# Two attention heads issued alternately on the two halves of TensorE, and their softmax made two heads ahead

## The reference, cut to what matters

```python
def hybrid_mixer(h, w_in, sink, conv_w, g_attn, g_conv, w_out, cos, sin):
    proj = h @ w_in                                   # 1024 -> 512 q, 128 k, 128 v, 3 x 512 gates
    q, k, v, gate_b, gate_c, u = jnp.split(proj, SPLITS, axis=-1)
    q = partial_rope(q.reshape(b, s, 8, 64), cos, sin)
    k = partial_rope(k.reshape(b, s, 2, 64), cos, sin)
    y_attn = windowed_gqa_with_sink(q, k, v, sink)    # 8 heads of 64, 2 key heads, window 128
    y_conv = gate_b * centred_short_conv(gate_c * u, conv_w)
    y = jnp.concatenate([rmsnorm(y_attn, g_attn), rmsnorm(y_conv, g_conv)], axis=-1)
    return y @ w_out
```

## Time and profile before the change

| what | value |
|---|---|
| median of three runs | 1908.02 us |
| the profiled execution's own time | 1910.71 us |
| its span (first to last instruction) | 1909.0 us |
| TensorE busy over the span | 1840.7 us, 96% |
| VectorE busy | 854.2 us, 45% |
| ScalarE busy | 686.5 us, 36% |
| mean granted TensorE clock | 0.993 |
| first mixer of layer 0, first scores to the sums of squares | 41.45 to 101.06 us |
| first mixer of layer 1, the same | 618.08 to 677.67 us |
| experts of layer 0 and 1, DMA share in their middle | 1.01, at 427 GB/s |

### The profile page before, as it was taken

How to read it: one execution, slowest core, us unless ns; L and a number is a source line. 1 busy time by engine, 2 the same in 40 slices (tenths; PEclk the granted TensorE clock), 3 DMA queues, 4 the chain that set the end, 5 groups by cost and what they waited for, 6 DMA issues and landing times.

```text
span 1909.0 us, 28641 instructions
## 1 busy us (share of the span) xinstructions
PE 1840.7 (96%) x11394; PEld 1248.8 (65%) x11394; DVE 854.2 (45%) x1921; ACT 686.5 (36%) x1319; POOL 277.1 (15%) x249
## 2 busy tenths in 40 slices
PE   8999999999999999999999999999899999999998
PEld 8874444444447874444434436888899978888997
DVE  5863121211215862112211114566785655668755
ACT  5632111111114541111111113557674544576654
POOL 1500000000000500000000003972000057800000
PEclk9999999999999999999999999999999999999999
DMA  8569999999996469999999996452534845433353
GB/s 298 219 263 415 418 428 426 428 428 428 428 424 231 183 280 412 421 427 428 428 428 428 428 427 230 144 207 89 174 97 151 282 169 177 174 132 109 120 169 134
DMA packets 121432, 557.61 MB, mean 292 GB/s; under 512 B 5008, under 2 KB 49584, under 8 KB 96240
## 3 DMA queue, kind: packets, MB, share of 16 engines
q1 hardware_dynamic: 119696, 551.51, 72.8%
q10 hardware_dynamic: 1440, 4.36, 0.6%
q0 software_dynamic: 192, 0.30, 0.1%
HBM read 555.11 MB, written 1.05 MB: 291 GB/s over the span
## 4 chain that ended last, share of the span: by engine, by line
PE 57%; DVE 4%; DMA 3%; ACT 3%; issue 2%; POOL 0%; SPq 0%; POOLq 0%; DVEq 0%; ACTq 0%
PE bank L2395 7%; PE bank L2426 5%; PE bank L2544 3%; PE bank L2546 3%; PE bank L2545 3%; DMA ring<-w_up_dram 3%; PE bank L2523 3%; PE bank L2524 3%; PE bank L2525 3%; PE bank L2397 3%; PE bank L2630 3%; PE bank L2493 2%; PE bank L2126 2%; PE bank L2560 1%; PE bank L2369 1%
## 5 line engine op out<-in xcount | busy, mean ns | idle before, releaser
L2395 PE MATMUL bank<-ring,work 128*64 128x512 f32 x544 | 244.2, 604 | 10.3 <-issue 10.3
L1717 DVE TENSOR_TENSOR work<-work,bank 64x512 f32<-64x512 f32 x64 | 43.9, 686 | 440.5 <-ACT work L1041 440.5
L2397 PE MATMUL bank<-ring,work 128*64 128x512 f32 x512 | 228.8, 602 | 0.0
L801 POOL TENSOR_TENSOR stat<-stat,power 128x1 f32<-128x1 f32 (+1 forms) x18 | 10.8, 602 | 1450.9 <-DVE stat L1289 960.0
L853 POOL TENSOR_TENSOR w_lo<-ring,w_hi 128x512 fp32r<-128x512 f32 (+1 forms) x160 | 208.9, 1324 | 53.7 <-ACT w_hi L1091 50.8
L1041 ACT ACTIVATE work<-bank 64x512 f32<-64x512 f32 x64 | 37.9, 592 | 466.9 <-PE bank L2397 466.9
L1091 ACT CAST w_hi<-ring 128x512 fp32r<-128x512 f32 (+1 forms) x208 | 123.4, 606 | 121.6 <-PE bank L2546 81.5
L2426 PE MATMUL bank<-ring,work 128*64 128x512 f32 x480 | 155.8, 595 | 1.8 <-ACT work L1046 0.4
L2395 PEld LDWEIGHTS bank<-ring,work 128*64 128x64 f32 x544 | 73.5, 139 | 123.5 <-issue 121.6
L1937 DVE TENSOR_TENSOR w_lo<-ring,w_hi 128x512 fp32r<-128x512 f32 (+1 forms) x176 | 115.8, 678 | 75.6 <-ACT w_hi L1203 75.5
L1733 DVE SCALAR_TENSOR_TENSOR act_hi<-bank,stat,act_hi 128x512 fp32r<-128x512 f32 x64 | 48.0, 750 | 211.1 <-ACT act_hi L1051 211.1
(11 more groups left out here) (361 smaller groups left out, 4605.6 us busy)
## 6 DMA issues: line engine op xcount, KB each, us to landing
ring<-w_in_dram SPq DMA_DIRECT2D x34, 2048.0 KB, 9.0
ring<-w_gate_dram SPq DMA_DIRECT2D x34, 2048.0 KB, 20.4
ring<-w_up_dram SPq DMA_DIRECT2D x32, 2048.0 KB, 26.0
ring<-w_down_dram SPq DMA_DIRECT2D x30, 2048.0 KB, 25.5
ring_tail<-w_down_dram SPq DMA_DIRECT2D x18, 2048.0 KB, 23.4
work<-w_gate_dram SPq DMA_DIRECT2D x16, 2048.0 KB, 21.2
work<-w_up_dram SPq DMA_DIRECT2D x16, 2048.0 KB, 25.8
ring_tail<-w_up_dram SPq DMA_DIRECT2D x16, 2048.0 KB, 27.0
```

The lines of the kernel that those rows point to most:

```text
L2395: pe.matmul(m_bank(m)[gate, :], lhs, wg[:, k], start=(k == 0), stop=(k == KD - 1), skip_group_check=True)
L2397: mu = pe.matmul(m_bank(m)[up, :], lhs, wu[:, k], start=(k == 0), stop=(k == KD - 1), skip_group_check=True)
```

## The change

The scores of two heads (h0, h0+1) are made by one function that issues their matmuls in turn, one on the upper half of the rows, one on the lower; the values of two heads likewise on the two halves of the columns, once both heads' transposes have been copied. The heads are taken in pairs: TensorE issues the scores of heads h+2 and h+3 before the transposes of an even head h, and the values of heads h-1 and h behind the tiles beside an odd head h. ScalarE and VectorE make the softmax two heads ahead: beside head h stand the logits, exponentials and weights of head h+2. On VectorE the logits are put before the work for the tiles beside the head and the weights behind it. The list of PSUM tiles follows TensorE's new order.

```diff
@@ psum_tiles
-        names += [("u", layer, 0), ("S1", layer, 0), ("u", layer, 1)]
+        names += [("u", layer, 0), ("S1", layer, 0), ("S1", layer, 1), ("u", layer, 1)]
         for h in range(HEADS):
-            names += [("S1", layer, h + 1)] if h + 1 < HEADS else []
+            names += [("S1", layer, h + 2), ("S1", layer, h + 3)] if h % 2 == 0 and h + 2 < HEADS else []
...
-            names += [("Y1", layer, h // 2)] if h % 2 == 0 else []
+            names += [("Y1", layer, h // 2)] if h % 2 == 1 else []
@@ ScalarE
                 round_chunks(gate_chunks(5))
+                exponentials(1)
                 done_tiles = 6
                 for hh in range(HEADS):
                     empty(("PT1", layer, hh), pT1[:, hh % 2].rearrange("p a b -> p (a b)"),
                           bank(("PT1", layer, hh))[:])
-                    if hh + 1 < HEADS:
-                        exponentials(hh + 1)
+                    if hh + 2 < HEADS:
+                        exponentials(hh + 2)
@@ VectorE
                 logits(0)
+                logits(1)
                 rest_of_chunks(layer, gate_chunks(4))
                 weights(0)
                 gated_input(0)
-                logits(1)
                 rest_of_chunks(layer, gate_chunks(5))
+                weights(1)
                 gated_input(1)
                 done_tiles = 6
                 for hh in range(HEADS):
                     if hh % 2 == 0 and hh > 0:
                         rest_of_y(hh // 2 - 1)
-                    if hh + 1 < HEADS:
-                        if hh > 0:
-                            logits(hh + 1)
-                        weights(hh + 1)
+                    if hh + 2 < HEADS:
+                        logits(hh + 2)
                     for nm, j in BESIDE_HEAD[hh]:
...
+                    if hh + 2 < HEADS:
+                        weights(hh + 2)
@@ TensorE
-                def scores(hh):
-                    name = ("S1", layer, hh)
-                    claim(name)
-                    r = slice(64 * (hh % 2), 64 * (hh % 2) + 64)
-                    kk = kT1[r, 0 if hh % 2 == hh // 4 else 1]
+                def scores(h0):
+                    for hh in (h0, h0 + 1):
+                        claim(("S1", layer, hh))
                     for qb in range(NT):
-                        mm = pe.matmul(bank(name)[:, qb * SEQ:(qb + 1) * SEQ], qT1[r, hh // 2, qb * P:(qb + 1) * P], kk,
-                                       start=True, stop=True)
-                    done(mm, name)
+                        for hh in (h0, h0 + 1):
+                            name = ("S1", layer, hh)
+                            r = slice(64 * (hh % 2), 64 * (hh % 2) + 64)
+                            kk = kT1[r, 0 if hh % 2 == hh // 4 else 1]
+                            mm = pe.matmul(bank(name)[:, qb * SEQ:(qb + 1) * SEQ], qT1[r, hh // 2, qb * P:(qb + 1) * P],
+                                           kk, start=True, stop=True)
+                            if qb == NT - 1:
+                                done(mm, name)
...
-                    if hh + 1 < HEADS:
-                        scores(hh + 1)
+                    if hh % 2 == 0 and hh + 2 < HEADS:
+                        scores(hh + 2)
...
-                    emptied(pe, ("PT1", layer, hh))
-                    yn = ("Y1", layer, hh // 2)
-                    if hh % 2 == 0:
+                    if hh % 2 == 1:
+                        emptied(pe, ("PT1", layer, hh - 1))
+                        emptied(pe, ("PT1", layer, hh))
+                        yn = ("Y1", layer, hh // 2)
                         claim(yn)
-                    r = slice(64 * (hh % 2), 64 * (hh % 2) + 64)
-                    v0 = QW + KVW + (hh // 4) * HD1
-                    for kb in range(NT):
-                        mm = pe.matmul(bank(yn)[r, 0:SEQ], qkv[:, kb, v0:v0 + HD1], pT1[:, hh % 2, kb],
-                                       start=(kb == 0), stop=(kb == NT - 1))
-                    if hh % 2 == 1:
+                        v0 = QW + KVW + (hh // 4) * HD1
+                        for kb in range(NT):
+                            for side in range(2):
+                                mm = pe.matmul(bank(yn)[64 * side:64 * side + 64, 0:SEQ], qkv[:, kb, v0:v0 + HD1],
+                                               pT1[:, side, kb], start=(kb == 0), stop=(kb == NT - 1),
+                                               skip_group_check=True)
                         done(mm, yn)
```

## The result

Five runs of the changed kernel took 1919.01 to 1924.09 us, median 1920.99; five of the kernel before on the same chip 1907.88 to 1911.76, median 1908.07. The ratio is 1.0058, 95% interval [1.0045, 1.007]: slower, by 12.9 us of median where the prediction had 5.6. The direction was right, the size was outside the range. The profiled execution after took 1919.44 us (span 1917.7, 8.7 more than before). It is a low one among its runs, and the profiled one of before (1910.71 us) a high one among its own, so the two traces can explain 8.7 of the 12.9 us.

The account below looks back on a forecast made before the run. The prediction took the VectorE-ScalarE softmax and rounding loop as the bound, about as long as TensorE's matmuls. Minus 16.6 matmul, plus 21.6 waiting, plus 0.6 clock gave +5.6 us: 1913.6 us as median, range 1910.4 to 1916.4.

Parts of the forecast that it names:

- Pairs: TensorE in the first two mixers: a pair costs what one costs, removing 8.3 us per layer, 16.6 in all.
- The new waits: VectorE beside heads: waits for ScalarE's rounding instead of exponentials, 9.6 us per layer against 8.1.
- Where TensorE is let go: Mixer's end: last hold moves to the output product's third weight chunk; sums of squares 2.5 us later per layer, bounds 1.2 to 3.1.
- The clock: TensorE's new idle stretches in the mixers may lower its clock: 0.6 us over two layers, bounds 0 and 6.8.
- a fall in both layers: Rival: the clock falls once or twice in each layer, adding 3.4 to 6.8 us, 1916.4 to 1919.8; chance 12%.
- Passing on: Behind the mixer up to the experts: the delay is passed on whole, two layers of 2.5, 5.0 us.
- From the profiled execution to the median: Whole kernel: 2.7 us taken off, as the median lay below the profiled run, giving 1913.6 from 1916.3.
- TensorE sets the pace: Rival, first mixers: softmax always in time, 18.2 us saved, 1889.8, or about 1900 in weak form; chance 13%.

Follow-up runs that it names:

- rounding_first: Changed kernel, with ScalarE rounding the first tile's chunks beside a head ahead of the exponentials; 1902.23 us, ratio 0.9958 to the kernel before.
- late_pairs: Changed kernel with softmax one head ahead as before, and each pair's scores issued at an odd head for the next two heads; 1909.57 us, ratio 0.9996.
- fillers_short: Changed kernel with 7 and 7 matmuls of zeros by ones in the two longest TensorE waits of each first mixer; 1916.81 us, ratio 1.0037.
- rf_apart_later: Changed kernel with rounding ahead of exponentials, scores and values one head at a time except the paired scores of heads 0 and 1; 1914.27 us, ratio 1.0037.
- pairs_back: Changed kernel with the two heads' score and value matmuls issued one head after the other; 1923.47 us, ratio 1.0066.

## Why the prediction was right in its sign and wrong in its size

1. *Pairs.* Right: 1.07 and 1.01 us a pair. The 10.05 us less busy TensorE in the 49 us of layer 0 are not all saved, since part of the work now lies behind that stretch. Over a whole mixer at a granted clock of 1.00, first that of layer 1 before, then that of rounding_first, it is 8.2 us for the 8.3 forecast:

```profile
618.08:677.67 59.59, 58.69 (x361) 47.42 (x361) 45.11 (x98) 36.21 (x93) 24.50 (x25) 1.00 0.53 212
613.40:667.98 54.58, 50.47 (x361) 43.03 (x361) 45.73 (x98) 35.77 (x93) 25.06 (x25) 1.00 0.58 231
```

   The "16 score matmuls" of the earlier trace rows are 16 records, so eight matmuls; the comparison with a lone group of four records stands. The Trainium skill warns that tiling does not speed up the emptying of PSUM (TensorEngine Tiling (Array Packing), Performance Considerations, PSUM Bottleneck). late_pairs, which has the pairs alone, agrees with it in the outcome (0.9996) and not in the cause: what bounds it is the loop of softmax and rounding (VectorE's 8.1 us of waits for exponentials), and no run here shows the emptying of PSUM as the bound.
2. *The new waits.* Right: 9.4 us in 6 waits for the rounding, where 9.6 was forecast, and 1.61 us in the turn shown.
3. *Where TensorE is let go: the first of two steps that failed, by its size.* The place was right, the third chunk of the first output tile. Forecast was 50.45 us behind the first scores, measured 51.01 (92.06 less 41.05): 0.56 short. What TensorE then has left was taken as 11.7 us; in fillers_short, at 2.4 GHz, it is 12.39, of which 0.66 is a wait for the convolution's rest that I had left out (VectorE makes it behind the same held-up low parts). So the term is 3.8 per layer and not 2.5, above my upper bound of 3.1: 2.5 + 0.56 + 0.66 makes 3.7 of it. Over two layers it was 2.6 us too small.
4. *The clock: the second step that failed, and by the medians the larger.* "I take a third of one such fall over the two layers, 0.6 us." The clock fell at the mixer's end in both layers of the trace, in layer 0 behind the idle stretches of 1.99 and 2.08 us, in layer 1 behind one of 1.97, and again in both routers. In the trace that cost 1.0 us in layer 0's mixer (64.44 for 63.4), nothing in layer 1's (63.41), and 3.5 in the routers, of which the experts of layer 0 gave back 1.5. By the runs it was about 4 us, the difference between the changed kernel and fillers_short. The third of a fall had no working behind it, and the earlier trace rows were too few: the trace of before has nine idle stretches of 2.17 to 2.27 us in the experts, and the clock fell behind six of them. Two of the six:

```profile
444.86 0.73 PE L2395 MATMUL bank<-ring,work 128*64 128x512 f32 x1 [2.23 <-issue]
...
532.95 0.61 PE L2395 MATMUL bank<-ring_tail,work 128*64 128x512 f32 x1 [2.25 <-issue]
```

```profile
443.00:451.00 8.00, 6.14 (x22) 2.44 (x24) 0.68 (x1) 0.28 (x1) 0.00 (x0) 0.79 1.01 430
531.00:539.00 8.00, 6.05 (x21) 2.34 (x23) 0.68 (x1) 0.34 (x1) 0.00 (x0) 0.79 1.00 426
```

   I gave the case of a fall in both layers 12% and made the other the forecast; its price of 3.4 to 6.8 was about right.
5. *Passing on.* Right in the sum: the mixers' 8.64 us are nearly the span's 8.73, because what the routers took (3.46) and what the experts gave back (2.54) nearly cancel. In layer 0 both are the clock. In layer 1 the clock fell three times in the experts both before and after, so their 1.07 us have another cause, which stays open.
6. *From the profiled execution to the median.* Taking off 2.7 us presumed that the profiled run after would stand to its median as that of before does. It stood 1.55 below it. That is 4.2 of the 12.9 us, and it overlaps with point 4, whose 4 us are taken from medians. The clock may be in it: the granted clock was 0.990 in the traced run and in that of 1919.01 us, 0.988 to 0.989 in the three slower ones, and 0.001 of the span is 1.9 us, an estimate for matmuls that are the bound. Where it fell in those runs no trace shows, so the cause stays open.

With terms 3 and 4 as measured the sum is 1908.0 + 2 x 3.8 + 4 = 1919.6, for 1921.0.

The rival "TensorE sets the pace" named the condition under which the pairs pay: VectorE's new waits short. rounding_first made them so, by another order on ScalarE, and the time came to 1902. With rounding first and without pairs the mixer takes 60.6 us, with both 54.6, with pairs alone and the softmax one head ahead 59.6. The rounding first with the softmax one head ahead was not run, so what the second head ahead is worth by itself is not shown.

Left open: why the clock falls in the router with the changed order and not before, with the same work and the same idle 0.6 us there. It fell there, in one layer or both, in the traces of all runs but the kernel before, late_pairs and rf_apart_later. Cutting that idle time to 0.23 us, or shortening the fillers, did not help.

## What to carry to other kernels

Ahead of a saving on one engine, find the loop that the others run among themselves: the same 7 to 8 us of matmul per layer were worth 0 in the old order, under 3 in the changed one and 6 once ScalarE rounded first. When work is moved ahead in time, look at what each engine does first in its turn: it should be what another engine needs next, and not what was moved. And a change that trades matmul time for idle time on TensorE should be priced with its clock: count in the trace how often such a stretch was followed by a fall, and charge the fall where TensorE sets the pace, or fill the stretch, with fillers measured in records.

## What the hardware showed that I had not expected

- *Halves run side by side in whatever order they are issued.* Scores of two heads, four records on one half of the rows and then four on the other, took 1.07 us to the next group, as when they alternate. In pairs_back the first record of the second head starts 0.013 us after the first of the first head, and the record that ends the first head's scores is the seventh of the eight to start; so the strict order in each engine's stream, of which the text on the kernel before speaks, does not hold for the starts of matmuls on different halves. That the Trainium skill calls the tiles independent, in loading and in matmul (TensorEngine Tiling (Array Packing), Key Properties), agrees with it. Between the values of one head and the scores of the next, one on halves of the columns and one on halves of the rows, there was no such overlap: 1.01 and 1.06 us, one behind the other.
- *A lower clock can move.* Before, the granted clock of layer 0 was 1.00 in the router and fell in the first experts; after, it fell in the router and held in the first experts. The same work of the first experts before, then after, where it stands 7.0 us later:

```profile
146.00:154.00 8.00, 6.70 (x30) 3.10 (x32) 2.47 (x10) 1.00 (x3) 0.00 (x0) 0.79 1.01 429
```

```profile
153.00:161.00 8.00, 6.72 (x36) 3.43 (x38) 3.23 (x11) 1.48 (x3) 0.00 (x0) 1.00 1.02 433
```

  The router takes 2.5 us longer with it and the experts 1.5 less, and three attempts to stop the fall in the router gained nothing that the times can tell. The 18 traces have 36 such layers. In 26 the clock fell between the router's transposes and the first expert; in nine of the other ten it fell in the first experts, 47 to 48 us behind the sums of squares; only layer 1 of the kernel before has neither. Why one of the two falls nearly always comes is not shown.
